# The last pair of experts in quarters of the inner columns, its last down rows by halves of the output

## What is computed

```python
xin = h[bidx, idx]                       # 64 tokens for each of 16 experts
hid = silu(einsum("becd,edf->becf", xin, w_gate)) * einsum("becd,edf->becf", xin, w_up)
y = einsum("becf,efd->becd", hid, w_down) * gates[..., None]
return zeros_like(h).at[bidx, idx].add(y)
```

## Time and profile before

| | |
|---|---|
| runs | 2430.46, 2432.68, 2436.47 us; median 2432.68 us |
| span of the profiled execution, first to last instruction | 2426.0 us |
| median less that span | 6.7 us |
| PE busy | 2284.4 us (94%) |
| DVE, ACT, POOL busy | 1058.7, 653.6, 210.6 us |
| bytes moved | 594.41 MB |
| granted TensorE clock, mean | 0.985 |

### The profile page before, as it was taken

One profiled execution on the slowest core, in us unless ns is written; L12 is line 12 of the kernel. 1 busy time (PEld: TensorE's weight loads), 2 busy tenths in 40 slices (PEclk: granted clock), 3 DMA queues, 4 the chain that ended last, 5 costly groups with the idle time before them and its releaser, 6 DMA issues.

```text
span 2426.0 us, 25175 instructions
## 1 busy us (share of the span) xinstructions
PE 2284.4 (94%) x10601; PEld 1443.1 (59%) x10601; DVE 1058.7 (44%) x1630; ACT 653.6 (27%) x1063; POOL 210.6 (9%) x185
## 2 busy tenths in 40 slices
PE   6999999999999999999989999999989898989888
PEld 4677657888888888888768567343323333323222
DVE  5987676756654666564766535010101010101001
ACT  4233464332332423323545642101000000000000
POOL 4332020000000000000312330100000000000000
PEclk8999999999999999999999999999999999999999
DMA  8332324555542355540311207999999999999998
GB/s 333 109 104 70 139 87 156 176 189 196 197 143 72 120 191 184 180 157 22 106 36 53 96 36 310 401 430 431 430 430 430 430 431 431 431 430 430 431 431 341
DMA packets 124454, 594.41 MB, mean 245 GB/s; under 512 B 10882, under 2 KB 12432, under 8 KB 98998
## 3 DMA queue, kind: packets, MB, share of 16 engines
q1 hardware_dynamic: 120866, 583.18, 60.7%
q0 software_dynamic: 3168, 9.50, 1.2%
q10 hardware_dynamic: 308, 0.13, 0.0%
HBM read 590.65 MB, written 2.14 MB: 244 GB/s over the span
## 4 chain that ended last, share of the span: by engine, by line
PE 78%; DMA 14%; DVE 5%; ACT 2%; issue 1%; SPq 0%; POOL 0%; DVEq 0%; ACTq 0%
PE PS L1405 15%; PE PS L1133 12%; PE PS L1080 10%; PE PS L1082 10%; PE PS L1081 10%; PE PS L176 5%; PE PS L1427 4%; DMA RING<-in_w_down_dram 2%; PE PS L1442 2%; DMA RING<-in_w_gate_dram 2%; PE PS L708 1%; DMA RB_a<-in_w_up_dram 1%; DMA RB_a<-in_w_down_dram 1%; DMA HID_e<-in_w_gate_dram 1%; DMA XT<-in_w_gate_dram 1%; DMA RB_a<-in_w_gate_dram 1%
## 5 line engine op out<-in xcount | busy, mean ns | idle before, releaser
L1405 PE MATMUL PS<-RING,HID_e 128*64 128x512 f32 x576 | 205.5, 608 | 9.0 <-DMA RING<-in_w_gate_dram 5.4
L1405 PE MATMUL PS<-RB_a,HID_e 128*64 128x512 f32 x576 | 204.4, 605 | 8.0 <-DMA RB_a<-in_w_up_dram 5.4
L2928 DVE TENSOR_TENSOR TMP<-TMP,PS 128x512 f32<-128x512 f32 x32 | 19.8, 682 | 370.3 <-PE PS L1405 370.3
L696 POOL TENSOR_TENSOR WPL_e<-RING,WPH_e 128x512 fp32r<-128x512 f32 x104 | 145.8, 1413 | 300.3 <-ACT WPH_e L1516 300.3
L1405 PE MATMUL PS<-HID_e 128*64 128x512 f32 x320 | 146.0, 606 | 5.8 <-DMA HID_e<-in_w_gate_dram 2.6
L1405 PE MATMUL PS<-AT_g,HID_e 128*64 128x512 f32 x288 | 130.3, 601 | 7.3 <-DMA AT_g<-in_w_up_dram 4.7
L2069 ACT ACTIVATE HID_e<-PS,cmat 128x128 f32<-128x128 f32 x32 | 12.0, 456 | 463.7 <-PE PS L176 463.7
L1405 PE MATMUL PS<-XT,HID_e 128*64 128x512 f32 x288 | 128.6, 595 | 5.3 <-DMA XT<-in_w_gate_dram 2.7
L1133 PE MATMUL PS<-AH_e,WPH_e 128*128 128x512 f32 x320 | 128.2, 401 | 4.8 <-DVE AL_e L2284 4.0
L1133 PE MATMUL PS<-AL_e,WPH_e 128*128 128x512 f32 x320 | 126.7, 396 | 0.0
L1405 PEld LDWEIGHTS PS<-RING,HID_e 128*64 128x64 f32 x576 | 61.3, 139 | 95.5 <-issue 81.6
(11 more groups left out here) (485 smaller groups left out, 4925.4 us busy)
## 6 DMA issues: line engine op xcount, KB each, us to landing
RING<-in_w_gate_dram SPq DMA_DIRECT2D x18, 2048.0 KB, 22.1
RB_a<-in_w_gate_dram SPq DMA_DIRECT2D x18, 2048.0 KB, 22.1
RB_a<-in_w_up_dram SPq DMA_DIRECT2D x18, 2048.0 KB, 18.1
RING<-in_w_down_dram SPq DMA_DIRECT2D x18, 2048.0 KB, 22.1
RB_a<-in_w_down_dram SPq DMA_DIRECT2D x18, 2048.0 KB, 22.1
RING<-in_w_up_dram SPq DMA_DIRECT2D x17, 2048.0 KB, 17.0
RING<-in_mlp_w_dram SPq DMA_DIRECT2D x32, 1024.0 KB, 5.3
RB_a<-in_mlp_w_dram SPq DMA_DIRECT2D x32, 1024.0 KB, 5.2
```

Of the source, the lines that this page charges most:

```text
L696: pool.tensor_tensor(WPL[:, n % 4, :], ring.view(*parts[b][1:], k // 4)[:, k % 4, :], WPH[:, n % 4, :].bitcast(F32), ALU.subtract).then_in ...
L1405: last = pe.matmul(b[64 * d:64 * d + 64, :], xv_[:, k, 64 * d:64 * d + 64], wv, start=k == 0, stop=k == 7)
L2928: dve.tensor_tensor(q, q, banks.of("up", n, fg), ALU.mult).then_inc(*V_moe.up("act", n, fg))
```

## The change

Pairs 0 to 6 stay. Pair 7 gets programs of its own on all engines.

The 2048 inner columns are taken in four quarters q of 512. For each quarter SP loads gate and up as one block each, now all eight channel rows of a partition but only 512 columns (`(8, 512)`: eight stretches of 2 KB in place of one of 16 KB). Down rows are grouped by the same quarters; those of quarters 0 and 1 are blocks with stretches of 16 KB as before, and stand behind the up block of quarters 1 and 2. The down rows of quarters 2 and 3 are loaded by halves of the output columns, first half 0 of both quarters, then half 1 of both, in stretches of 2 KB.

PE works through gate and up of a quarter in one bank each, turns a quarter when its product is there, and takes the down rows half by half at the end. The scatter of pair 6 stands between the first four steps of quarter 0. After half 0 of the output is summed, DVE weights it, PE scatters it and DVE adds it, between the two quarters' rows of half 1; after half 1 the same again. SP stores the four pieces of half 0 and then the four of half 1.

```diff
+        last_pieces = (((2, 0, 4, 0), (3, 0, 4, 1)), ((2, 0, 4, 2), (3, 0, 2, 3), (3, 2, 4, 4)))
+
         def sp_experts(sp, w):
-            for n in range(8):
+            for n in range(7):
                 for m in range(2):
                     for kp in range(4):
                         if (n, m, kp) == (0, 1, 0):
@@ -506,17 +508,27 @@
                                      (T_moe, "gu", n, m, kp))
                             if extra:
                                 big.many, big.i = 7, 0
-                for kq in range(4 if n < 7 else 2):
+                for kq in range(4):
                     for d in range(2):
                         rows8 = A["w_down_2"][0, 2 * n + d].rearrange("(h p k) n -> h p k n", h=2, k=8)
                         big.load(sp, w, ("dn", n, kq, d), rows8[kq // 2, :, 4 * (kq % 2):4 * (kq % 2) + 4, :], (4, 1024),
                                  (T_moe, "dn", n, kq))
-            for kq in (2, 3):
-                views = [big.claim(w, ("dn", 7, kq, d), (4, 1024), (T_moe, "dn", 7, kq)) for d in range(2)]
-                for k in range(4 * kq - 8, 4 * kq - 4):
+            rows4 = [A["w_down_2"][0, 14 + d].rearrange("(q p k) n -> q p k n", q=4, k=4) for d in range(2)]
+            for q in range(4):
+                for m in range(2):
                     for d in range(2):
-                        rows8 = A["w_down_2"][0, 14 + d].rearrange("(h p k) n -> h p k n", h=2, k=8)
-                        sp.dma_start(views[d][:, k % 4, :], rows8[1, :, k, :]).then_inc(*D[f"last{2 * k + d}"].up())
+                        rows8 = A[("w_gate_2", "w_up_2")[m]][0, 14 + d].rearrange("(p k) n -> p k n", k=8)
+                        big.load(sp, w, ("gu", 7, m, q, d), rows8[:, :, 512 * q:512 * q + 512], (8, 512),
+                                 (T_moe, "gu", 7, m, q))
+                if q in (1, 2):
+                    for d in range(2):
+                        big.load(sp, w, ("dn", 7, q - 1, d), rows4[d][q - 1], (4, 1024), (T_moe, "dn", 7, q - 1))
+            for hf in range(2):
+                views = [big.claim(w, ("dn", 7, "last", hf, d), (8, 512)) for d in range(2)]
+                for q, k0, k1, i in last_pieces[hf]:
+                    for d in range(2):
+                        sp.dma_start(views[d][:, 4 * q - 8 + k0:4 * q - 8 + k1, :],
+                                     rows4[d][q, :, k0:k1, 512 * hf:512 * hf + 512]).then_inc(*D[f"last{2 * i + d}"].up())
...
-            for i in range(4):
-                for hf in range(2):
+            for hf in range(2):
+                for i in range(4):
                     w.wait_ge(*V_moe.at("sc", 7, i, hf))
                     sp.dma_start(out[0, i * 128:(i + 1) * 128, hf * 512:(hf + 1) * 512],
...
+                pe_scatter_half(pe, w, n, i, hf, 4 + (2 * i + 2 + hf) % 4)
+
+        def pe_scatter_half(pe, w, n, i, hf, seat):
+            b = banks.seat(w, seat, ("sc", n, i, hf), (V_moe, "sc", n, i, hf))
+            w.wait_ge(*V_moe.at("y", n, hf))
+            pe.matmul(b, PTm[n % 2][:, i * 128:(i + 1) * 128], yB[:, hf * 512:(hf + 1) * 512], start=True,
+                      stop=True).then_inc(*T_moe.up("sc", n, i, hf))
+
...
+        def pe_last_pair(pe, w):
+            def columns(m, q):
+                b = (banks.seat(w, 2 + q % 2, ("up", 7, q), (V_moe, "act", 7, q)) if m else
+                     banks.seat(w, q % 2, ("gate", 7, q), (S_moe, "silu", 7, q)))
+                for k in range(8):
+                    w.wait_ge(*(S_moe if k > 3 else V_moe).at("x", 7, k))
+                    for d in range(2):
+                        w.wait_ge(*big.landed("gu", 7, m, q, d))
+                        last = pe.matmul(b[64 * d:64 * d + 64, :], xins[1][:, k, 64 * d:64 * d + 64],
+                                         big.view("gu", 7, m, q, d)[:, k, :], start=k == 0, stop=k == 7)
+                    if (m, q) == (0, 0) and k < 4:
+                        pe_scatter(pe, w, 6, k)
+                last.then_inc(*T_moe.up("gu", 7, m, q))
+
+            def turn(q):
+                b = banks.seat(w, 6 + q % 2, ("hid", 7, q), (S_moe, "hid", 7, q))
+                w.wait_ge(*V_moe.at("act", 7, q))
+                transposes(pe, b, [hidden[:, 512 * q + j:512 * (q + 1):4] for j in range(4)]).then_inc(
+                    *T_moe.up("hid", 7, q))
+
+            def rows(q, k, hf, wv, landed):
+                w.wait_ge(*S_moe.at("hid", 7, q))
+                for d in range(2):
+                    w.wait_ge(*landed(d))
+                    last = pe.matmul(bs[hf][64 * d:64 * d + 64, :], hidT[:, 4 * q + k, 64 * d:64 * d + 64], wv(d),
+                                     start=q == 0 and k == 0, stop=q == 3 and k == 3)
+                return last
+
+            def whole(q):
+                for k in range(4):
+                    for hf in range(2):
+                        last = rows(q, k, hf, lambda d: big.view("dn", 7, q, d)[:, k, 512 * hf:512 * (hf + 1)],
+                                    lambda d: big.landed("dn", 7, q, d))
+                last.then_inc(*T_moe.up("dn", 7, q))
+
+            def half(q, hf):
+                for p, k0, k1, i in last_pieces[hf]:
+                    for k in range(k0, k1) if p == q else ():
+                        last = rows(q, k, hf, lambda d: big.view("dn", 7, "last", hf, d)[:, 4 * q - 8 + k, :],
+                                    lambda d: D[f"last{2 * i + d}"].all())
+                if q == 3:
+                    last.then_inc(*T_moe.up("down", hf))
+
+            for q in range(4):
+                columns(0, q)
+                if q:
+                    turn(q - 1)
+                columns(1, q)
+                if q == 0:
+                    bs = [banks.seat(w, 4 + hf, ("down", 7, hf), (V_moe, "y", 7, hf)) for hf in range(2)]
+                elif q < 3:
+                    whole(q - 1)
+            half(2, 0)
+            turn(3)
+            half(3, 0)
+            half(2, 1)
+            for i in range(4):
+                pe_scatter_half(pe, w, 7, i, 0, (6, 7, 0, 1)[i])
+            half(3, 1)
+            for i in range(4):
+                pe_scatter_half(pe, w, 7, i, 1, (2, 3, 6, 7)[i])
...
-            for n in range(8):
+            for n in range(7):
                 pe_up(pe, w, n)
                 pe_down(pe, w, n)
-            for i in range(4):
-                pe_scatter(pe, w, 7, i)
+            pe_last_pair(pe, w)
...
+            for q in range(4):
+                h = hid_tmp.seat(w, q, ("hid", 7, q), (T_moe, "hid", 7, q))
+                w.wait_ge(*T_moe.at("gu", 7, 0, q))
+                act.activation(h, banks.of("gate", 7, q), ACT.Silu, bias=0.0, scale=1.0).then_inc(*S_moe.up("silu", 7, q))
+                if q:
+                    act_moe_hidden(act, w, 7, q - 1)
+            act_moe_hidden(act, w, 7, 3)
...
                 for hf in range(2):
-                    dve.tensor_tensor(yB[:, hf * 512:(hf + 1) * 512], banks.of("down", n, hf),
-                                      g2b[:, hf * 512:(hf + 1) * 512], ALU.mult).then_inc(*V_moe.up("y", n, hf))
-            dve_scatter(dve, w, 7)
+                    dve_weighted(dve, w, n, hf)
+            dve_scatter(dve, w, 6)
+            for q in range(4):
+                h = hid_tmp.of("hid", 7, q)
+                w.wait_ge(*S_moe.at("silu", 7, q))
+                w.wait_ge(*T_moe.at("gu", 7, 1, q))
+                dve.tensor_tensor(h, h, banks.of("up", 7, q), ALU.mult).then_inc(*V_moe.up("act", 7, q))
+            w.wait_ge(*T_moe.at("sc", 6, 3, 1))
+            for hf in range(2):
+                w.wait_ge(*T_moe.at("down", hf))
+                dve_weighted(dve, w, 7, hf)
+                for i in range(4):
+                    dve_scatter_half(dve, w, 7, i, hf)
```

More of the change, by code:

```diff
@@ L246, in build_program @@
         D = {n: signal(f"landed_{n}", 16) for n in
-             ("id", "fw", "cm", "x", "dft", "rope", "brow", "band", "rb", "scr", "bg", "blk", "tri", "br", "out", "wr", "gp", "wg", *(f"last{i}" for i in range(16)),
+             ("id", "fw", "cm", "x", "dft", "rope", "brow", "band", "rb", "scr", "bg", "blk", "tri", "br", "out", "wr", "gp", "wg", *(f"last{i}" for i in range(10)),
               "vec0", "vec1", "vec2", "gb0", "gb1", "gb2", "gb3")}
@@ L1423, in pe_down @@
                     for d in range(2):
-                        w.wait_ge(*(D[f"last{2 * (k - 8) + d}"].all() if n == 7 and k > 7 else
-                                    big.landed("dn", n, k // 4, d)))
+                        w.wait_ge(*big.landed("dn", n, k // 4, d))
                         wv = big.view("dn", n, k // 4, d)[:, k % 4, 512 * hf:512 * (hf + 1)]
@@ L2101, in act_experts @@
             act_gather(act, w, 0)
-            for n in range(8):
-                if 0 < n < 7:
+            for n in range(7):
+                if n:
                     act_gather(act, w, n + 1)
@@ L2867, in dve_scatter, with dve_scatter_half, dve_weighted @@
                 for hf in range(2):
[L2868 to L2871, removed]
```

(9 more changed lines are left out.)

## The result

| | before | changed |
|---|---|---|
| median of 12 runs each | 2433.31 us | 2440.15 us |
| lowest, highest | 2427.69, 2437.13 | 2431.70, 2444.45 |
| ratio of the runs | | 1.0027, 95% interval 1.0014 to 1.0039 |
| span of the profiled execution | 2426.0 us | 2440.6 us |

The change makes the kernel slower by 6.6 us (3.4 to 9.5), 0.27%. Forecast were 2440.4 us and +7.7.

What follows compares the result with a forecast made beforehand. The prediction took the full DMA queue as the bound in the last stage. Gate and up blocks +6.7, last two blocks +1.7 and tail -0.6 gave +7.7 us on 2432.68, so 2440.4 us; range 2433.5 to 2449.

Steps and rivals of the forecast that it cites:

- What bounds the kernel: Last stage: loads set the time, 9.73 us a block at 431 GB/s, while PE needs 7.09 us.
- The bytes, 0.83 us a block: Eight gate and up blocks of pair 7 in 2 KB stretches: 397 GB/s, 10.56 us a block, 0.83 more.
- The last two blocks at 389: Last two down blocks, 2 KB of 4 KB rows: 389 GB/s, 10.78 us each, +1.7 us in landing.
- Slots and SP cost nothing: Pair 7 loads: SP's issue and the buffer slots keep the DMA queue full; slot cover at least 12 us, cost nothing.
- PE's list, 33.9 us: From the last up block's landing to the end of the span: PE's work, add and store take 33.93 us.
- PE is late by nearly 5: At the last landing: PE finishes its down rows nearly 5 us after the bytes have come.
- The tail, -0.6 us: Behind the last landing: 12.4 us where 13.0 lay, a gain of 0.6 us.
- the chain through the last up block: Sign in the new profile: the chain of waits runs through the last up block, not through the last load.
- A: Rival: short stretches cost little or nothing; +0.7 us at 431 GB/s, +5.0 at 409; chance 0.28.
- B: Rival: a slower stream of short stretches, 353 GB/s, +19.9 us, 2452.6 us; chance 0.15 for under 385.
- C: Rival: PE's clock falls after a wait; 1.7 us more if at the last up block, 2442.1 us; chance 0.15.
- The 0.3% line: Whole kernel: measurement tells about 0.3%, 7.3 us, from no change; the forecast, 0.32% up, stands just past it.

Runs made afterwards that it cites:

- all_4k: The kernel before, with gate and up loads of pairs 1 to 7 in stretches of 4 KB: 2445.90 us, ratio 1.0053.
- all_2k: The kernel before, with gate and up loads of pairs 1 to 7 (56 blocks) in stretches of 2 KB: 2482.40 us, ratio 1.0204.
- tail_only: The kernel before, with only the last two down blocks of pair 7 by output halves in 2 KB stretches: 2436.99 us, ratio 1.0003.
- whole_gu: The changed kernel, with each gate and up load of pair 7 in whole 16 KB stretches: 2432.81 us, ratio 1.0002 to the kernel before.
- again_c: The changed kernel a second time, no edit: 2442.07 us, ratio 1.0032 to the kernel before.

## Why the prediction was right, point by point

**What bounds the kernel.** Right: with all else as in the change, giving the loads their 16 KB back takes away 5.1 of the 6.1 us.

**The bytes, 0.83 us a block.** Right in kind. The size was a choice between 409, 397 and 389 GB/s; the landings in the second profile of the changed kernel give 407 (10.31 us a block, +0.58), and the seven pairs give 0.89 a block over 4 runs, which is 395. 397 lies between, but for the kernel that was forecast 407 counts. It lies outside the forecast's own 389 to 404. The landing of the last up block was forecast 104.0 us after T0 and came after 102.1. The reason I gave for 397, rows of 8 KB between rows of 4 and of 16, was only argued: all_4k and all_2k show that the length of a stretch counts at one pitch, and nothing here tests the pitch. The Trainium skill's account of a fixed overhead for each packet ("DMA: Bandwidth & Descriptors", section Why small descriptors are slow (HBM only)) gives, by the same estimate as in the prediction, 424 GB/s for 4 KB and 414 for 2 KB. The 4 KB blocks of all_4k, 416 to 421 by estimate, lie a little under it, and the changed kernel's 407 further under its 414.

**The last two blocks at 389.** Too dear. PE's waits in tail_only show the first block and a half landing in 15.4 us (2401.5 to 2416.8), which is 409 GB/s, though these rows are 4 KB. Forecast were 16.2.

**Slots and SP cost nothing.** Right: the DMA share is 1.04 over pair 7, SP had the last up block issued 13.9 us before it landed, and whole_gu, in the same order, has its blocks 9.7 us apart.

**PE's list, 33.9 us, and "PE is late by nearly 5".** Measured 34.3 and 34.1. The terms one by one: 7.02 and 3.43 as forecast, the turn with its copy 1.36 in place of 1.83 (the 1.13 us row that I took for one turn has eight transposes, two turns; one is 0.69. A transpose is recorded once, not twice as said of the matmuls above), two halves 7.45 to 7.52 in place of 7.25, the rest within 0.2. PE finished its rows at 2433.6, 5.9 us after the last landing, where 4.9 were forecast.

**The tail, -0.6 us.** This term is of the wrong sign. The last piece was issued at 2416.75 in the second profile and took 11.0 us to land, so 13.5 us stand behind the last landing at 2427.7, where 12.4 were forecast and 13.0 stood before. PE's list was sized well; the bytes were there a microsecond sooner than by 389, and that microsecond is nothing gained.

**The sum.** From T0, second profile against before:

| term | forecast | measured |
|---|---|---|
| last up block lands (before, at its place: the second down block, 97.3 us after T0) | +6.7 us | +4.8 |
| the last two blocks (before: 19.9 us) | +1.7 | +0.9 |
| behind the last landing (before: 13.0 us) | -0.6 | +0.5 |
| together | +7.7 | +6.2 |

Two terms were too high and the third too low, so that the sum is nearer than its terms. With 407 GB/s for all the short stretches the forecast's own steps give 2295.8 + 82.5 + 19.5 + 33.56 = 2431.4, +5.4 us. That 2440.4 fell within 0.3 us of the median 2440.15 is luck: the forecast starts from a median of 2432.68 for before, and the runs beside the changed kernel had 2433.31. What is right without luck is the mechanism, the sign and the order of size. Of the signs that were named, the chain through the last up block came; the rate, the 10.5 us between blocks and the 12 to 13 us behind the last landing each missed by a little.

**The rivals.** A at 409 GB/s gave +5.0: with the tail as it was it would have been close, and the profile sides with its rate more than with mine. In the runs the two can't be told apart. A's upper end, the full rate, for which the Trainium skill's 512 bytes ("DMA: Bandwidth & Descriptors", section Specifications) were named, is refuted by whole_gu: with whole stretches the same kernel is 5.1 us shorter. B, 353 GB/s, didn't come, though 368 occurred for 10 us in all_2k. C came, at the last gate block of the first profile (granted clock 0.73 from 2396 to 2406): 2.6 us longer where 1.7 were priced, and nearly all hidden by the wait for the last up block, since from T0 this execution is only 0.3 longer than the other.

**The 0.3% line.** The forecast stood past it and the measured 0.27% just short of it; the interval, 0.14 to 0.39%, holds both.

## What to carry to other kernels

Where a full DMA queue is the bound, the length of the contiguous stretch is part of the work: here 16, 4 and 2 KB ran at 431, about 420 and 407 GB/s (2 KB down to 384 over one pair), so a finer split that makes PE's tail shorter must first earn back what its stretches cost over all the blocks it cuts. Before work is moved ahead of the last bytes, ask whether the engine that does it has time there: moved into a list that is already late, it only moves other work back. And read two profiles from a common event that lies ahead of the change, not from their spans.

## What the runs showed that I had not expected

The part of the program ahead of pair 7 took 2295.5 to 2304.9 us in ten profiles of kernels that are equal up to there; that spread of 9 us is larger than the effect studied. The spread goes with the granted clock: the three profiles with T0 at 2295.5 to 2295.8 have a mean clock of 0.984 or 0.985, the seven with T0 at 2300.4 to 2304.9 have 0.979 to 0.982. The clocks differ ahead of the experts (from 1200 to 1300 us 0.95 in the profile of before and 0.91 in that of the changed kernel); from 1600 us to T0 both move 430 to 431 GB/s. The timed runs do the same: in the 29 runs of before beside again_c, the six at a clock of 0.985 or more took 2424.96 to 2428.47 us, the fourteen at 0.980 or less 2431.66 to 2438.56. The changed kernel's four runs at 0.985 took 2431.70 to 2435.87, so its cost shows at like clocks too. What makes the clock differ from run to run isn't shown.

Blocks of 2 KB stretches, at a DMA share of 1.04, moved 368 GB/s in one window of 10 us and, by estimate, 400 to 409 in windows of 100 and 200 us.
